# Later-opening row buffers, and attention steps moved from ahead of block 0's scores to behind them, in one fused hybrid decoder layer

## The reference

```python
merged = g_conv * conv_y + g_swa * (swa_o @ w_swa_out) + g_mem * (mem_o @ w_mem_out)
x = x + merged @ w_out
x = x + peer_ffn(rmsnorm(x, norm2_g), peer_w_q, peer_keys, peer_w_down, peer_w_up)

def one_block(xb):                      # 128 tokens
    q = (xb @ w_q).reshape(PEER_BLOCK, PEER_HEADS, 2, PEER_DK_HALF)
    s = jnp.einsum('thcd,hcnd->thcn', q, keys, preferred_element_type=jnp.float32)
    sv, si = lax.top_k(s, PEER_TOPK)
    cand = (sv[:, :, 0, :, None] + sv[:, :, 1, None, :]).reshape(PEER_BLOCK, PEER_HEADS, PEER_TOPK * PEER_TOPK)
    cv, ci = lax.top_k(cand, PEER_TOPK)
    ...
    eid = i0 * PEER_N_KEYS + i1
    gate = jax.nn.softmax(cv, axis=-1)
    u = w_down[eid]
    act = jax.nn.gelu(jnp.einsum('td,thkd->thk', xb, u, preferred_element_type=jnp.float32), approximate=False)
    return jnp.einsum('thk,thkd->td', (gate * act).astype(xb.dtype), w_up[eid])
```

## Time and profile before

| what | value |
|---|---|
| median of 3 runs | 3355.59 us (3354.1 to 3359.14) |
| span of the profiled execution | 3347.1 us |
| TensorE busy | 3087.0 us (92%) |
| VectorE busy | 2512.8 us (75%) |
| ScalarE busy | 779.2 us (23%) |
| GpSimd busy | 1611.7 us (48%) |
| DMA, mean over the span | 322 GB/s |
| row gathers (L1404), w_down | 1024 |
| w_up steps, 512 KB each | 512 |

### The profile page before, as it was taken

How to read it: one execution, slowest core, us unless ns; L and a number is a source line. 1 busy time by engine, 2 the same in 40 slices (tenths; PEclk the granted TensorE clock), 3 DMA queues, 4 the chain that set the end, 5 groups by cost and what they waited for, 6 DMA issues and landing times.

```text
span 3347.1 us, 33154 instructions
## 1 busy us (share of the span) xinstructions
PE 3087.0 (92%) x11349; PEld 1818.7 (54%) x11349; DVE 2512.8 (75%) x5082; ACT 779.2 (23%) x2063; POOL 1611.7 (48%) x1269
## 2 busy tenths in 40 slices
PE   8999798998989999779999999999999999997874
PEld 5677687866847654445545445545545545543321
DVE  2298434986889789888988888888888868455556
ACT  2001542321310114324214204204204214200000
POOL 0000002545145677745566667557657657444434
PEclk9999899999998999899999999999999999998998
DMA  3111466999599999999999999999999999899998
GB/s 130 43 37 58 147 204 231 336 334 354 197 339 351 359 404 397 331 368 370 381 353 388 357 380 388 344 389 385 358 377 380 359 400 373 335 410 393 408 410 316
DMA packets 326171, 1077.16 MB, mean 322 GB/s; under 512 B 40468, under 2 KB 73877, under 8 KB 325340
## 3 DMA queue, kind: packets, MB, share of 16 engines
q0 software_dynamic: 172416, 625.03, 48.7%
q1 hardware_dynamic: 119275, 428.87, 34.1%
q10 hardware_dynamic: 34312, 21.16, 2.0%
HBM read 1052.50 MB, written 23.94 MB: 322 GB/s over the span
## 4 chain that ended last, share of the span: by engine, by line
PE 29%; DMA 20%; DVE 15%; issue 13%; POOL 10%; ACT 1%; ACTq 1%; DVEq 0%; POOLq 0%
PE psum L1666 17%; DMA arena<-in_w_down,arena 12%; POOL arena L1404 9%; DMA arena<-in_w_up,arena 7%; DVE arena L2019 5%; PE psum L1469 4%; PE psum L1642 2%; PE psum L1529 2%; PE psum L1513 1%; ACTq L2264 1%; PE psum L1612 1%; DVE arena L2113 1%; DMA arena<-scratch_s 1%; DMA arena<-in_w_q 1%; PE psum L1515 1%
## 5 line engine op out<-in xcount | busy, mean ns | idle before, releaser
L1404 POOL DMA_INDIRECT arena<-in_w_down,arena x1024 | 1419.2, 1386 | 735.5 <-DVE arena L2019 503.1
L1666 PE MATMUL psum<-arena 128*128 128x512 f32 x3584 | 1602.0, 598 | 77.1 <-DMA arena<-in_w_up 70.8
L2019 DVE CUSTOM_DVE_ANT_0 arena<-arena 128x1024 f32<-128x1024 f32 x1024 | 1220.0, 1222 | 256.3 <-DMA arena<-in_w_down,arena 247.8
L1666 PEld LDWEIGHTS psum<-arena 128*128 128x128 f32 x3584 | 664.4, 191 | 871.0 <-issue 734.3
L1513 PE MATMUL psum<-arena 128*128 128x256 f32 (+2 forms) x1536 | 361.6, 390 | 17.0 <-DVEq L1831 5.5
L2321 ACT ACTIVATE arena<-arena 128x128 f32<-128x128 f32 x896 | 285.6, 390 | 323.8 <-DVE arena L2043 314.7
L2043 DVE TENSOR_TENSOR arena<-constants,arena 128x1024 f32<-128x1024 f32 x224 | 273.4, 1224 | 77.7 <-PE psum L1469 65.0
L1513 PEld LDWEIGHTS psum<-arena 128*128 128x128 f32 x1536 | 267.9, 195 | 99.5 <-issue 13.3
L1469 PEld LDWEIGHTS psum<-arena 128*128 128x128 f32 x1792 | 237.8, 195 | 153.2 <-ACT arena L2321 86.6
L1469 PE MATMUL psum<-arena 128*128 128x128 f32 x1792 | 245.0, 281 | 40.4 <-ACT arena L2321 40.2
L2113 DVE SCALAR_TENSOR_TENSOR arena<-arena 128x1024 f32<-128x1024 f32 x128 | 164.4, 1284 | 122.6 <-DMA arena<-in_w_up,arena 121.3
(11 more groups left out here) (317 smaller groups left out, 2039.8 us busy)
## 6 DMA issues: line engine op xcount, KB each, us to landing
arena<-in_w_up SPq DMA_DIRECT2D x512, 512.0 KB
arena<-in_w_gates SPq DMA_DIRECT2D x96, 768.0 KB
arena<-in_w_o SPq DMA_DIRECT2D x40, 512.0 KB
arena<-in_w_q SPq DMA_DIRECT2D x32, 512.0 KB
arena<-in_w_down,arena POOLq DMA_INDIRECT x1024
arena<-in_w_chunks SPq DMA_DIRECT2D x26, 512.0 KB, 3.5
arena<-scratch_s POOLq DMA_DIRECT2D x64, 128.0 KB
scratch_s<-arena ACTq DMA_DIRECT2D x11, 512.0 KB
```

The source lines that it names most:

```text
L1404: pool.indirect_dma_start(dst, None, table, bass.IndirectOffsetOnAxis(ap=idN[:, min(n, NT - 1) % 2, j:j + 1], axis=0)).then_inc(here, 16)
L1666: mm = pe.matmul(psum[:, 2 * (m % 2) + h, :], coef_block(m, s % NKEYS), wup[s % WUPR][:, h * 512:(h + 1) * 512], start=first, stop=end)
L2019: dve.tensor_tensor_reduce(row, row, rowD[slot_of["x", n]], 1.0, 0.0, ALU.mult, ALU.add, dots[:, n % 3, j:j + 1]).then_inc(row_used, 1)
```

## The change

Two tables are changed; nothing of the computation is.

```diff
-        items = att(0) + mixed(pairs_of(0, 0)[0:6], range(1, 6), 1) + pairs_of(0, 0)[6:] + mixed(pairs_of(0, 1, 2), range(6, 10), 4)
+        items = att(0) + mixed(pairs_of(0, 0)[0:6], range(1, 6), 1) + pairs_of(0, 0)[6:] + pairs_of(0, 1, 2)
         pr = pairs_of(1, 0)
-        items += pr[0:1] + outs(0, 0) + att(10) + pr[1:2] + att(11) + turns([0]) + pr[2:3] + queries(0) + scores([0])
-        items += mixed(pr[3:] + pairs_of(1, 1, 2), range(12, 18), 3)
+        items += outs(0, 0) + att(6) + pr[0:1] + att(7) + turns([0]) + pr[1:2] + queries(0) + scores([0])
+        items += mixed(pr[2:], range(8, 12), 1) + mixed(pairs_of(1, 1, 2), range(12, 18), 2)
...
-        open_from = [0] * 5 + [184] * 4 + [KEPT] + [122] * 3 + [2] + [80] * 2 + [0] * 2 + [190] * 2
+        open_from = [0] * 5 + [230] * 4 + [KEPT] + [160] * 3 + [2] + [80] * 2 + [0] * 2 + [215] * 2
```

## The result

The changed kernel took 3376.32 us (median of 6 runs, 3367.45 to 3387.57), the kernel before 3353.01 beside it; the ratio is 1.0079, with a 95% interval of 1.0061 to 1.0096: by the ratio some 26 us slower (the two medians are 23 us apart). Forecast were 3352.5 us and no measurable difference; the time lies just above the range that was given (3330 to 3376). The profiled execution of the changed kernel (3382.09 us) is itself 6 us above its median.

A forecast was written before the change was run, and what follows sets the result against it. TensorE, busy 92% of the span, was taken to set the time overall, with the end bound by DMA; 29 us late less 32 at the end gave -3, span 3344 plus 8.5 outside, 3352.5 us; range 3330 to 3376.

The forecast's parts named there:

- Block 0's scores earlier: Four attention stages and one pair leave the front of block 0's scores; first key search 21.3 us earlier, at 526 us.
- Up to block 1's residual: From block 0's first key search, 40 us more VectorE work; residual at 743 instead of 724.6 us, 19 us late.
- if none of that idle time is filled: Before block 1's residual, VectorE's 12 idle us stay: 19 us late; if all is filled, 7; 19 was taken.
- 725 to 931 us: From block 1's residual, 6 us come back, then 8 are added and about 5 absorbed; next output product 16 us late.
- 931 to 1613 us: Up to the w_up steps, 20 us late behind the last pair, then 6 and some 3 more; 29 us late in all.
- My sum without absorption: At the last pair, 16 + 14 = 30 us late; 17 if lateness fills VectorE's 13.4 us wait; 20 was taken.
- The end: Behind the w_up steps, DMA-bound, 24 rows less to bring; 32 us earlier.
- What lies outside the span: Time added to the forecast span of 3344 us to get the kernel's time; 8.5 us.
- The slower one: Rival: too few open buffers for rows 122 to 159, 20 us of row waits; net +17, 3372.6 us, chance 0.25.
- The estimate of 3.2 us a row: Against the slower rival: by the skill's fit five buffers give a row in 0.93 us, below the dot's time.
- The rule on repeated gaps: Repeated gaps on the engine that should be full can mean too few open buffers; by it the slower rival's time.

The follow-up runs named there:

- after_pairs2: Changed kernel with att(8) to att(11) begun three pairs behind block 0's scores instead of one; 3353.99 us, ratio 1.0009 to the kernel before.
- items_only: Kernel before with only the changed list of TensorE items, buffers opening at the rows of before; 3382.62 us, ratio 1.0103.
- open_only: Kernel before with only the changed rows from which buffers open, items as before; 3344.77 us, ratio 0.9998.
- late_only: Kernel before with LATE open from row 230 instead of 184, XB3 and XB4 from 215 instead of 190; 3333.34 us, ratio 0.9969.
- late230: Kernel before with LATE alone open from row 230 instead of 184, XB3 and XB4 staying at 190; 3340.61 us, ratio 0.9975.

## Why the prediction was wrong

In short: the work was counted rightly and so was the end; what failed, at three places, is the treatment of waits. The prediction took idle time as something that new work leaves as it is or fills, and lateness as something that waits absorb. The runs showed added waits (idle time of VectorE 26 us for 12 up to block 1's residual) and next to no absorption behind it, so the fifth sum came 67 us late, not 29.

**Block 0's scores earlier: right.** Of 21.3 us, 20.3 came at the first key search and 19.1 at the scores themselves. The 1 us for the output product behind the last pair of group 0 did come (1.06 us in the changed kernel) and is part of what is missing.

**Up to block 1's residual: the work right, the waits missing.** VectorE's 40 us more were 39. The step that failed is "if none of that idle time is filled": I asked how much of the idle time the new work would fill and did not ask what it would add. Idle went from 12 us to 26 and the residual to 33 us late, not 19. What VectorE waited for in this stretch, before (547 to 725 us):

```profile
DVE arena L2019 <- DMA arena<-in_w_down,arena: 3.8, 4, 2.2
DVE arena L1821 <- ACT arena L2189: 2.1, 4, 0.9
```

and after (527 to 758 us):

```profile
DVE arena L1821 <- ACT arena L2189: 11.2, 6, 3.7
DVE arena L2019 <- DMA arena<-in_w_down,arena: 7.4, 6, 2.8
```

Nine of the 14 us are for ScalarE's step on the gate products (L2189), which itself comes behind TensorE's product and VectorE's adds of the pair two before; so what makes TensorE late comes back to VectorE. The place was to be seen before: VectorE waits 33.6 us for the first scores, and the order of the list shows the attention stage right behind the scores. The prediction took that idle time as a sign that VectorE "is ready". For the key search it was; but it is not free for what stands behind the waiting step in its own list, and there the move put an attention stage's maxima. Of the 25 us that after_pairs2 takes back at the residual, this first wait is some 4; most are the ten rows and the head search that the planner drew in with this order, whose work the prediction had counted. So the failed term is the 14 us of added waits.

**725 to 931 us: 16 forecast, 40 measured.** The 6 us given back were 9.5 (33 late to 23.5). The stretch behind it grew by 17 us, not 8: VectorE was busy for 101.75 us, 15 more than the earlier trace rows where 12.7 were worked out, and idle for 13, not 6 (10 before). The 5 us that a pair and the w_o wait were to absorb at 940 us were not there: TensorE was as late as VectorE, 40 us.

**931 to 1613 us: the worst of it.** My sum without absorption was 30, of which the 13.4 us wait for ScalarE was to be filled. It grew:

```profile
1184.61 0.56 DVE L1828 TENSOR_TENSOR arena<-arena,psum 128x384 f32<-128x384 f32 x1 [20.32 <-ACT arena L2189]
```

ScalarE's step (L2189) stands behind its own issues of the scores' writes (L2264). Before:

```profile
1117.70 20.13 ACTq L2264 DMA_DIRECT2D scratch_s<-arena  x2
```

and after:

```profile
1165.37 18.61 ACTq L2264 DMA_DIRECT2D scratch_s<-arena  x2
```

They ended 46 us later, and VectorE came to its wait 39 us later, so its lateness did not use this wait up. From the output product of blocks 3 and 4 to that behind the last pair the lateness grew by 25 us and I had 4. In items_only it did not grow there (39 to 37), in open_only by 13: it goes with the opening rows, with or without the items. The further 9 us up to the fifth sum were 2; two of the nine are a slip, since the prediction's own counts give ten rows less there (254 to 244), not eight.

**The end: right.** 32 us forecast, 33 to 34 measured from the fifth sum on; the order of the list told the 24 rows and DMA the price. The runs bear the price out up to 996 rows and not beyond, which the prediction did not say.

**What lies outside the span.** I took 8.5 us from one span and a median. For the changed kernel's profiled execution, 3382.09 us with a span of 3380.4, it is 1.7 us; the rest was the spread of single executions. With 1.7 the forecast would have been 3345.7 us, further off.

**The rivals.** The slower one gave 3372.6 us, near the measured 3376, and that is luck: the sign of its mechanism was to be 20 us or more of row waits in 834 to 960 us, and in 857 to 972 us they are 3.8. Row waits did grow elsewhere, from 92 to 115 us in all up to the first sum, 15 of it in 980 to 1185 us; but open_only, with the same buffers, loses nothing. The estimate of 3.2 us a row, from the fit in the Trainium skill's "DMA: Bandwidth & Descriptors", section "Anatomy of one DMA — SWDGE (gpsimd) path", spoke against this rival, and the rival did not come about. But the trace does not bear the 3.2 us out, and not the 4.43 us of the first row either. The page of the profile after has, over all rows, the median from issue to landing:

```profile
arena<-in_w_down,arena POOLq DMA_INDIRECT x1024, 8.3
```

and in 857 to 972 us it is 7.3 us. By the prediction's formula five buffers would then give a row in (7.3 + 1.15 + 0.3) / 5 = 1.75 us, more than a dot's 1.15. This did not matter, because VectorE took only 41 rows in these 115 us, one in 2.8 us. The step that failed in this rival is the comparison with the time of one dot.

The rule on repeated gaps in the Trainium skill's "Perfetto Trace Analysis", section "Optimization Strategy", names SBUF and PSUM. The prediction applied it to the row buffers, and there it is not what happened. The gaps that did repeat on TensorE (34.7 us in 10 waits, 21.5 in 3) are for VectorE to be done with a pair in PSUM, which is the other case that the rule names; whether more room in PSUM would have closed them no run shows.

So the chance of 0.25 for a slower kernel was too low for another reason: waits were counted too small and then hoped to absorb the lateness. By place, the 38 us between 29 and 67 are 14 at block 1's residual, 10 from there to the output product of blocks 3 and 4, 20 to that behind the last pair, less 6 from there on.

## What to carry to other kernels

When a step is moved behind the point at which another engine waits for data, read that engine's list: idle time in an in-order list is no free time for what stands behind the wait. Run the parts of a change alone: here one part of it was a gain, one a loss, and their sum hid both. Count lateness on an engine that sets the pace at its full size from joint to joint, and take something off only where a row shows that the other side is not late too. Rows brought earlier past one buffer's first fill are only a gain if they also get past the next one, which is to be looked up in the same table. Whether few buffers suffice is a question of how often a row is needed, not of how long one dot takes.

## What was not expected of the hardware

Two kernels with the same row counts at every step looked at (late_only and late230) had profiled spans of 3317.7 and 3345.4 us, while their ratios agree (0.9969 and 0.9975). TensorE and POOL have the same order in both, and VectorE's differs in three places, by a row each. Between block 1's first dense matrix and the fifth sum late_only took 1336 us and late230 1348, where before took 1358. TensorE's waits for ScalarE (L2321) were 5.9 us in the one and 18.4 in the other, which is these 12 us; why they differ is open. For a question of less than 10 to 20 us, ratios over many runs have to answer, not one trace.

A row of 512 KB took 8.3 us from issue to landing in the changed kernel (the median of 1024), where the first row had been used 4.43 us after its issue in before.
